# Two transformer blocks on one core: the second buffer of transposed activations at the same offset within 512 bytes as the first

## Chip, core and metric

One core of a Trainium2 chip runs the whole program as one launch. The metric is the device time of that core in microseconds (us). All operands are fp32 in memory. The engines are named as in the profile: PE is TensorE (matmuls), PEld its weight loads, DVE is VectorE, ACT is ScalarE, POOL is GpSimd, SP is SyncE, whose queue issues the DMAs.

## What is computed

256 tokens of width 2048 go through three layers. What matters here are the dense products, since they fill PE:

```python
def _layer(x, ...):                      # first block
    proj = rmsnorm(x) @ w_in             # 2048 -> 2560, then attention and a state space mixer
    x = x + mixed @ w_out                # 2048 -> 2048
    return x + (silu(h2 @ w_ff_gate) * (h2 @ w_ff_up)) @ w_ff_down     # hidden 5632

def second_block(x, ...):                # two more layers
    mix = gmlp_shortconv_mixer(hn, w_in_ab, ..., w_out_ab)             # layer 0: 2048 -> 5120 -> 2048
    mix = dilated_attention_mixer(hn, w_qkv, w_o, positions)           # layer 1
    h = h + rmsnorm(mix, ...)
    f = jnp.square(jax.nn.relu(rmsnorm(h, ...) @ w_up)) @ w_down       # both layers, hidden 8192
    h = h + rmsnorm(f, ...)
```

## The kernel before

**Split products.** Each fp32 product is made of three fp32r matmuls on split operands. A weight tile of 128 rows by 1024 columns is loaded into `RAW` (3 slots of two such tiles, `NRAW`), ACT rounds it into `HI` (L576) and DVE writes the rest into `LO` (L1063), both with 3 slots (`NSPLIT`). The activations are split likewise: they are transposed on PE (L1909, `feed`), ACT writes the rounded part and DVE the rest into a buffer of transposed activations.

**Two such buffers.** `KPA` and `KPB` have the same shape, 128 partitions by 16 chunks by 2 parts (rounded, rest) by 256 tokens, 32768 bytes a partition. `KPA` holds what goes into the products of the normed input (`w_in`, gate and up, `w_in_ab`, `w_qkv`, `w_up`), into `w_glu` and into the state space half of the first `w_out`. `KPB` holds what goes into the products that lead back to the stream: the attention half of the first `w_out`, `w_ff_down`, `w_out_ab`, `w_o` and `w_down`. For the hidden layers `KPB` is used as two halves, chunks 0 to 7 and chunks 8 to 15, in turn (blocks `hid1.b` and `hid2.layer.b`, even and odd b), and the program alternates: one `up` unit from `KPA`, then two `dn` units from `KPB`.

**One step.** `matmuls(u, i)` (L1860 to L1888) does chunk i of unit u: for each of the two tiles t of 128 tokens the three products rounded x HI, rounded x LO, rest x HI, each with 512 columns for the two halves j of the 1024, so 12 matmuls a step (8 read HI, 4 read LO; all are L1884). The 128x128 activations are the stationary operand, one piece of 512 bytes a partition at `buffer + 2048*chunk + 1024*part + 512*t`; the weights `HI`, `LO` are the moving operand, 2048 bytes a partition. A step needs one tile of HI, one of LO and half a DMA of 1 MB.

**Order.** Each engine's instructions are written out in program order by Python generators; semaphores join them. ACT and DVE run ahead of PE by two steps (`LA`) and then wait for a slot of HI or LO. Nothing in the order depends on addresses.

**Layout.** `build` places the SBUF tensors one behind the other from `SBUF_FROM` (16512) up, each rounded up to 64 bytes; the bytes under 16384 are a scratch area that the program builder reserves for descriptors of DMAs generated in software. In bytes of a partition, with the offset within 512 behind: `XR` 16512 (128), `KPA` 32896 (128), `RAW` 65664 (128), `HI` 90240 (128), `LO` 102528 (128), `ACC` 114816 (128), then small ones (`PAR`, `ID`, `ST`, `NEG5`, `LAM`), whose sizes are not multiples of 512, `KPB` 134912 (256), and behind it from `ph_at` 167680 (256) the area that the stages share (`HS`, `JK`, `RL`, `GPF`, `q2T`, `k2T`, `LG`, `PT`, `CL` and others). `BLT` and the bias tables lie inside `KPB`'s bytes while it is not in use.

Of the kernel before, what the change touches and what calls it, by code (L numbers as in the profile page):

```python
# [21 lines left out]
NRAW = 3  # L22
NSPLIT = 3
LA = NSPLIT - 1
SBUF_FROM = 16512
SBUF_TO = 229344


# [268 lines left out]
def program(nc, inp, out, scratch):  # L297
    plan = Plan(inp)
    with ExitStack() as ctx:
        build(nc, ctx, plan, inp, out, scratch)  # L300


def build(nc, ctx, plan, inp, out, scratch):
    S = Semaphores(nc, ctx)
    PS = ctx.enter_context(nc.psum_tensor("PS", [128, 8, 512], F32))
    U, G = plan.by_name, plan.groups
    at = [SBUF_FROM]

    def sb(name, shape, dt=F32, where=None):
        w = where if where is not None else at  # L310
        n = 4
        for d in shape[1:]:
            n *= d
        h = nc.alloc_sbuf_tensor_at(name, list(shape), dt, offset=w[0])
        w[0] += -(-n // 64) * 64
        assert w[0] <= SBUF_TO, (name, w[0])
        return h

    XR = sb("XR", [128, 2, D])
    kpa_at = at[0]  # L320
# [7 lines left out]
    ST = sb("ST", [128, 384])  # L328
    NEG5 = sb("NEG5", [128, 48])
    LAM = sb("LAM", [128, 3, 32])  # L330
    kb = [at[0]]
    ph_at = at[0] + 32768
    BLT = sb("BLT", [128, 4, 2, 8, 128], where=kb)
# [21 lines left out]
    PHI = sb("PHI", [128, 2, 512], where=third)  # L355
    xr_again = [SBUF_FROM]
    LANE = [[sb(f"LANE{p}{i}", [128, 512], where=xr_again) for i in range(2)] for p in range(2)]
# [71 lines left out]
    sp = {n: SPR[:, i, :] for i, n in enumerate("mag qf fre fim dt ang v1 v2 v3 v4 v5 v6 q4".split())}  # L429
    lre, lim, rho = (LAM[:, i, :] for i in range(3))  # L430

# [2023 lines left out]
```

## Time and profile before

| | |
|---|---|
| median of 3 runs | 3388.08 us (3386.37 to 3388.2) |
| the profiled execution, its own time | 3388.41 us |
| its span in the trace | 3386.3 us |
| PE busy | 3273.7 us, 97% |
| DVE, ACT, POOL busy | 1866.3, 1475.8, 119.8 us |
| DMA | 596.28 MB, mean 176 GB/s |

The span is the stretch that the trace covers; the run's time has 2.1 us more around it. Ends of matmuls are modelled in the trace, so a matmul's duration (some 390 ns) is longer than its share of PE: the time that one takes from PE is the distance from its start to the next one's start, which is called pace here.

### The profile page before, as it was taken

To read this page: it belongs to the slowest core of one execution; us is meant where nothing else is said; L and a number is where in the kernel's file an instruction comes from. 1 tells how busy PE (TensorE), PEld (TensorE's weight loads), DVE (VectorE), ACT (ScalarE), POOL (GpSimd) and SP (SyncE) were. 2 spreads that over 40 slices of the span, in tenths; PEclk is the share of its full clock that TensorE was granted. 3 is DMA by queue.
4 is the path that set the end of the run, shared out by engine and by line. 5 is a ranking of instruction groups with operands and counts; after the bars stand their busy time and mean duration, and the time that the engine had idled before them with its cause. 6 is when DMAs were issued, how large, how long until landed. Compare 5 with 4: busy or idle time off the path is not lost. (4 is left out here: it accounts for less than half of the span.)

```text
span 3386.3 us, 38632 instructions
## 1 busy us (share of the span) xinstructions
PE 3273.7 (97%) x15842; PEld 2670.4 (79%) x15842; DVE 1866.3 (55%) x1958; ACT 1475.8 (44%) x1760; POOL 119.8 (4%) x99
## 2 busy tenths in 40 slices
PE   6988999999999999999999999999999999999998
PEld 5776788888888778878888888878787788888886
DVE  6455655555555544665555555565555655555555
ACT  5434444444444444444444444444444544444443
POOL 4230000000000000000000000000000000000000
PEclk9998999999999999999999999999999999999999
DMA  7233455555555555555555555545454555555554
GB/s 200 93 119 121 159 187 186 188 188 193 189 186 187 181 172 188 194 174 180 191 188 190 186 187 186 185 156 186 149 174 154 173 184 186 187 187 187 187 188 146
DMA packets 187548, 596.28 MB, mean 176 GB/s; under 512 B 12491, under 2 KB 19308, under 8 KB 186860
## 3 DMA queue, kind: packets, MB, share of 16 engines
q1 hardware_dynamic: 187372, 593.82, 53.9%
q8 instruction: 125, 2.05, 0.2%
q14 instruction: 51, 0.42, 0.0%
HBM read 588.54 MB, written 5.23 MB: 175 GB/s over the span
## 5 line engine op out<-in xcount | busy, mean ns | idle before, releaser
L1063 DVE TENSOR_TENSOR LO<-RAW,HI 128x1024 fp32r<-128x1024 f32 (+1 forms) x1104 | 1351.6, 1226 | 1183.2 <-ACT HI L576 1181.4
L576 ACT ACTIVATE HI<-RAW 128x1024 fp32r<-128x1024 f32 (+1 forms) x1104 | 1159.2, 1052 | 1396.5 <-PE PS L1884 1392.1
L1884 PE MATMUL PS<-HI,KPA 128*128 128x512 f32 x5376 | 1499.4, 395 | 18.0 <-issue 5.3
L1884 PEld LDWEIGHTS PS<-HI,KPA 128*128 128x128 f32 x5376 | 1008.5, 190 | 233.4 <-issue 15.8
L1884 PE MATMUL PS<-HI,KPB 128*128 128x512 f32 x3392 | 954.9, 397 | 3.9 <-DVE ACC L1559 3.3
L1884 PE MATMUL PS<-LO,KPA 128*128 128x512 f32 x2688 | 841.4, 394 | 9.9 <-DVE LO L1063 9.8
L1884 PEld LDWEIGHTS PS<-HI,KPB 128*128 128x128 f32 x3392 | 631.6, 188 | 150.5 <-issue 5.2
L1884 PEld LDWEIGHTS PS<-LO,KPA 128*128 128x128 f32 x2688 | 509.0, 190 | 122.2 <-DVE LO L1063 11.9
L1884 PE MATMUL PS<-LO,KPB 128*128 128x512 f32 x1696 | 533.9, 395 | 0.8 <-DVE KPB L1099 0.8
L1884 PEld LDWEIGHTS PS<-LO,KPB 128*128 128x128 f32 x1696 | 318.8, 188 | 77.5 <-issue 1.2
L603 ACT ACTIVATE KPB<-PS 128x512 fp32r<-128x512 f32 x98 | 58.6, 599 | 185.0 <-PE PS L1909 185.0
L1094 DVE TENSOR_TENSOR KPB<-PS,KPB 128x512 fp32r<-128x512 f32 x98 | 67.7, 692 | 124.2 <-ACT KPB L603 124.2
L1727 POOL TENSOR_TENSOR ST<-ST,NEG 128x2 f32<-128x2 f32 (+2 forms) x15 | 19.8, 1322 | 2909.7 <-DVE ST L1106 2909.5
L1099 DVE SCALAR_TENSOR_TENSOR KPA<-PS,PAR,KPA 128x256 fp32r<-128x256 f32 x104 | 45.3, 479 | 61.2 <-ACT KPA L608 61.1
L1557 DVE TENSOR_TENSOR ACC<-PS,ACC 128x1024 f32<-128x1024 f32 x60 | 70.7, 1216 | 8.8 <-PE PS L1884 8.8
L608 ACT ACTIVATE KPA<-PS,PAR 128x256 fp32r<-128x256 f32 x104 | 43.3, 470 | 61.2 <-PE PS L1909 60.8
L1909 PE MATMUL PS<-ID,XR 128*128 128x128 f32 x192 | 33.7, 304 | 24.8 <-DVE XR L1591 15.6
L1618 DVE TENSOR_TENSOR HS<-RL 128x1024 f32<-128x1024 f32 x32 | 39.2, 1226 | 25.6 <-ACT RL L979 23.9
L1909 PEld LDWEIGHTS PS<-ID,XR 128*128 128x128 f32 x192 | 26.3, 156 | 33.0 <-DVE XR L1591 19.2
L1909 PEld LDWEIGHTS PS<-ID,HS 128*128 128x128 f32 x344 | 42.8, 140 | 12.0
L1909 PE MATMUL PS<-ID,HS 128*128 128x128 f32 x344 | 51.5, 272 | 0.0
L979 ACT ACTIVATE RL<-PS,ST 128x1024 f32<-128x1024 f32 x32 | 35.8, 1119 | 27.5 <-DVE HS L1618 22.7
(255 smaller groups left out, 988.2 us busy)
## 6 DMA issues: line engine op xcount, KB each, us to landing
RAW<-in_w_up SPq DMA_DIRECT2D x128, 1024.0 KB, 5.1
RAW<-in_w_down SPq DMA_DIRECT2D x128, 1024.0 KB, 5.5
RAW<-in_w_qkv SPq DMA_DIRECT2D x48, 1024.0 KB, 5.1
RAW<-in_w_ff_gate SPq DMA_DIRECT2D x88, 512.0 KB, 3.7
RAW<-in_w_ff_up SPq DMA_DIRECT2D x88, 512.0 KB, 4.6
RAW<-in_w_ff_down SPq DMA_DIRECT2D x44, 1024.0 KB, 5.5
RAW<-in_w_in_ab SPq DMA_DIRECT2D x40, 1024.0 KB, 5.0
RAW<-in_w_in SPq DMA_DIRECT2D x16, 1024.0 KB, 6.2
```

Source lines behind the costliest of these rows:

```text
L576: e.activation(HI[:, s % NSPLIT, 0:w], RAW[:, d % NRAW, j, 0:w], ACT.Copy).then_inc(S("hi_made"), 1)
L603: e.activation(kt[:, ks:ks + 2, 0, :], PS[:, bank, :].rearrange("p (a b) -> p a b", a=2), ACT.Copy).then_inc(S("chunk_hi"), 1)
L608: ins = e.activation(kt[:, ks + c, 0, :], PS[:, bank, c * 256:c * 256 + 256], ACT.Copy, scale=par(g.gain, 2 * j + c, 1))
L979: e.activation(RL[:, :], flat2(b), ACT.Relu, scale=r[:, t:t + 1]).then_inc(S("evac_act"), 1)
L1063: e.tensor_tensor(LO[:, h, 0:w], RAW[:, d % NRAW, j, 0:w], HI[:, h, 0:w].bitcast(F32), ALU.subtract).then_inc(S("lo_made"), 1)
L1094: e.tensor_tensor(kt[:, ks:ks + 2, 1, :], PS[:, bank, :].rearrange("p (a b) -> p a b", a=2), kt[:, ks:ks + 2, 0, :].bitcast(F32), ALU.subt ...
L1099: ins = e.scalar_tensor_tensor(out=kt[:, ks + c, 1, :], in0=PS[:, bank, c * 256:c * 256 + 256], scalar=par(g.gain, 2 * j + c, 1), in1=kt[: ...
L1557: ins = e.tensor_tensor(d, flat2(b), d, ALU.add)
L1618: e.tensor_tensor(HS[b % 2][:, t, :], RL[:, :], RL[:, :], ALU.mult).then_inc(S("squared_relu"), 1)
L1727: e.tensor_tensor(dst, src, NEG5[:, 0:n], ALU.pow).then_inc(S("root_made"), 1)
L1884: ins = e.matmul(PS[:, b + j, 0:cw], l, r[:, h, 512 * j:512 * j + cw], start=(i == 0 and part == 0), stop=(last and part == 2))
L1909: ins = e.transpose(PS[:, bank, c * 256 + t * 128:c * 256 + t * 128 + 128], src(2 * j + c, t), ID[:, :])
```

## The change

It gives the scratch area 4096 bytes in place of 16384, starts the kernel's tensors 12288 bytes lower (from 16512 to 4224), and spends 384 of the bytes that this frees on moving `KPB` up to the same offset within 512 bytes as `KPA`. No instruction, wait or DMA is added, removed or put elsewhere; only addresses differ, and line numbers (L1884 is then L1886).

```diff
-SBUF_FROM = 16512
+SCRATCH = 4096
+SBUF_FROM = SCRATCH + 128
 SBUF_TO = 229344
@@
     NEG5 = sb("NEG5", [128, 48])
     LAM = sb("LAM", [128, 3, 32])
+    at[0] += (kpa_at - at[0]) % 512
     kb = [at[0]]
     ph_at = at[0] + 32768
     BLT = sb("BLT", [128, 4, 2, 8, 128], where=kb)
@@
-    nc = _bacc.Bacc("TRN2", target_bir_lowering=False, num_devices=1)
+    nc = _bacc.Bacc("TRN2", target_bir_lowering=False, num_devices=1, dynamic_dma_scratch_size=SCRATCH)
```

What it makes of the addresses (bytes of a partition, offset within 512 behind):

| tensor | before | after |
|---|---|---|
| XR | 16512 (128) | 4224 (128) |
| KPA | 32896 (128) | 20608 (128) |
| RAW | 65664 (128) | 53376 (128) |
| HI | 90240 (128) | 77952 (128) |
| LO | 102528 (128) | 90240 (128) |
| ACC | 114816 (128) | 102528 (128) |
| ID | 132288 (192) | 120000 (192) |
| KPB | 134912 (256) | 123008 (128) |
| shared area, from ph_at | 167680 (256) | 155776 (128) |

After it `KPA`, `HI`, `LO` and `KPB` also have the same offset within 4096 bytes (128); before, `KPB` had 3840 there and the others 128.

## Rows read from the trace of the kernel before

**Rows 1.** The page: span, busy time by engine, granted clock in 40 slices.
```profile
span 3386.3 us, 38632 instructions
...
PE 3273.7 (97%) x15842; PEld 2670.4 (79%) x15842; DVE 1866.3 (55%) x1958; ACT 1475.8 (44%) x1760; POOL 119.8 (4%) x99
...
PEclk9998999999999999999999999999999999999999
```
**Rows 2.** Groups by line and shape: count, busy us, mean ns, idle before and releaser.
```profile
L1063 DVE TENSOR_TENSOR LO<-RAW,HI 128x1024 fp32r<-128x1024 f32 x1088 | 1337.9, 1232 | 1163.8 <-ACT HI L576 1162.0
L576 ACT ACTIVATE HI<-RAW 128x1024 fp32r<-128x1024 f32 x1088 | 1149.2, 1059 | 1367.9 <-PE PS L1884 1363.5 <-DMA RAW<-in_w_in 4.5
...
L1618 DVE TENSOR_TENSOR HS<-RL 128x1024 f32<-128x1024 f32 x32 | 39.2, 1226 | 25.6 <-ACT RL L979 23.9 <-PE PS L1884 1.7
```
**Rows 3.** The view of line L1884: count, shortest/median/longest duration in ns.
```profile
L1884 PE MATMUL PS<-HI,KPA x5376: 387/389/797, 10.3 to 3280.6; 128*128 128x512 f32 x200
...
L1884 PE MATMUL PS<-HI,KPB x3392: 387/395/763, 369.8 to 3371.9; 128*128 128x512 f32 x200
...
L1884 PE MATMUL PS<-LO,KPA x2688: 387/389/796, 11.5 to 3280.2; 128*128 128x512 f32 x192
...
L1884 PE MATMUL PS<-LO,KPB x1696: 390/393/628, 371.3 to 3371.5; 128*128 128x512 f32 x189
```
**Rows 4.** Timeline of PE in an up unit: start us, length us, what.
```profile
1060.12 1.07 PE L1884 MATMUL PS<-HI,KPA 128*128 128x512 f32 x4
...
1068.28 1.07 PE L1884 MATMUL PS<-HI,KPA 128*128 128x512 f32 x4
```
**Rows 5.** The same in a dn unit on chunks 8 to 15 of KPB.
```profile
1881.98 1.10 PE L1884 MATMUL PS<-HI,KPB 128*128 128x512 f32 x4
...
1894.58 1.10 PE L1884 MATMUL PS<-HI,KPB 128*128 128x512 f32 x4
```
**Rows 6.** The same in a dn unit on chunks 0 to 7 of KPB.
```profile
1790.52 1.10 PE L1884 MATMUL PS<-HI,KPB 128*128 128x512 f32 x4
...
1804.52 1.10 PE L1884 MATMUL PS<-HI,KPB 128*128 128x512 f32 x4
```
**Rows 7.** The same in the unit wa1, chunks 0 to 7 of KPB.
```profile
385.31 1.09 PE L1884 MATMUL PS<-HI,KPB 128*128 128x512 f32 x4
...
395.06 1.09 PE L1884 MATMUL PS<-HI,KPB 128*128 128x512 f32 x4
```
**Rows 8.** The same where an up unit ends and a dn unit begins.
```profile
1085.96 1.07 PE L1884 MATMUL PS<-HI,KPA 128*128 128x512 f32 x4
...
1087.32 0.62 PE L1884 MATMUL PS<-HI,KPA 128*128 128x512 f32 x2
1087.78 0.64 PE L1884 MATMUL PS<-HI,KPB 128*128 128x512 f32 x2
1088.25 0.62 PE L1884 MATMUL PS<-LO,KPB 128*128 128x512 f32 x2
```
**Rows 9.** Chain that ended last, one piece: the two units of w_o without transposes.
```profile
2593.90 44.89 PE PS L1884 x192
```
**Rows 10.** Stretches of an up unit and a dn unit: busy, PEclk, DMA share, GB/s.
```profile
1750.00:1760.00 10.00, 10.00 (x46) 8.29 (x45) 4.90 (x4) 3.67 (x4) 0.00 (x0) 1.00 0.56 175
...
1885.00:1895.00 10.00, 10.00 (x44) 8.06 (x43) 4.24 (x4) 4.24 (x4) 0.00 (x0) 1.00 0.56 175
```
**Rows 11.** The view of line L1909, transposes from the shared area and from XR.
```profile
L1909 PE MATMUL PS<-ID,HS x344: 270/272/273, 472.1 to 3299.3; 128*128 128x128 f32 x172
...
L1909 PE MATMUL PS<-ID,XR x192: 270/273/474, 6.5 to 2678.5; 128*128 128x128 f32 x192
```
**Rows 12.** The page, DMA queues: packets, MB, share of 16 engines.
```profile
q1 hardware_dynamic: 187372, 593.82, 53.9%
q8 instruction: 125, 2.05, 0.2%
q14 instruction: 51, 0.42, 0.0%
```

## The prediction

> **What bounds the kernel now.** I read the page first. PE is busy for 3273.7 of the 3386.3 us of the span, DVE and ACT for about half, and the granted clock is at its upper level (2.4 GHz) in nearly every slice [rows 1]. The groups say the same from the other side: DVE's LO instructions stood idle for 1163.8 us until ACT's HI was there, and ACT's HI for 1363.5 us until a matmul of L1884 had freed a slot [rows 2]. So the stream of dense matmuls sets the time, and ACT, DVE and the weight DMAs follow it. A saving on a dense matmul is then a saving on the run, as long as those three keep up.
>
> A change that only moves addresses can act there only by the time that one matmul takes. The view of the line shows a first trace of that: the median duration is 389 ns with KPA as the stationary operand and 395 (HI) or 393 (LO) with KPB, though all four groups do the same work [rows 3]. Durations have modelled ends, so I go on to the timeline and take the distance between starts. One half of a step is 6 matmuls, from one "HI x4" row to the next.
> - up unit on KPA, no other PE work between: (1068.28 - 1060.12) / 36 = 226.7 ns [rows 4].
> - dn unit on chunks 8 to 15 of KPB: (1894.58 - 1881.98) / 54 = 233.3 ns [rows 5]; on chunks 0 to 7: (1804.52 - 1790.52) / 60 = 233.3 ns [rows 6].
> - unit wa1 on KPB: (395.06 - 385.31) / 42 = 232.1 ns [rows 7].
> - the two w_o units without transposes, as a whole: (44.89 - 0.39) / 191 = 233.0 ns; 0.39 is the length of the last matmul [rows 3, 9].
>
> So each matmul whose stationary operand lies in KPB costs some 6 ns more. The clock is no part of it: it is 1.00 in both kinds of stretch, and DMA share (0.56) and GB/s (175) are alike [rows 10]. Nor is a late input: no row of these stretches has an idle time before it. At a border the pace goes over with the operand itself: up to 1087.32 the last 6 matmuls on KPA take 1.36 us, and the first 2 on KPB, with HI and LO made in the same way and the same work on ACT and DVE, take 0.47 us, 235 ns each [rows 8].
>
> **The change part by part.**
>
> *KPB from offset 256 to offset 128 within 512.* KPB is the stationary operand of 3392 + 1696 = 5088 dense matmuls [rows 3]. What tells KPB from KPA in the program is its address alone: shape, steps between pieces and type are the same, and HI and LO are read in the same way. In address, two things differ: the offset within 512 (256 against 128, with all of HI, LO, RAW at 128), and where in the partition it lies. The change takes the first difference away, and not the second. If the pace follows the offset, all 5088 go from 233.0 to 226.7 ns: 5088 x 6.3 ns = 32.1 us, all of it on PE, which sets the end. The bounds are 5.4 ns (232.1 - 226.7, rows 7), 27.5 us, and 6.6 ns (233.3 - 226.7, rows 5 and 6), 33.6 us. I take the value of rows 9 since it is that of whole units, not of a picked stretch.
>
> That piece of reasoning rests on rows alone, and a rule speaks against it. The Trainium skill says that TensorE has two independent read ports in SBUF, so that loading the next weights takes nothing from the running matmul (TensorE: Matmul & The Clock Gate, Step-by-step), that "PE and ACT never wait on anyone" (SBUF — State Buffer, Who interferes with whom), and that what counts for an access is its 16-byte line (the same page, the box on cachelines of Door 1); 128 and 256 are both multiples of 16. By these the offset could cost nothing and the sum would be 0 in place of -32.1. Against the trace that holds only half: the rule has no place for 233 beside 227, which the rows show, so something in the address does cost. It is kept as a rival below.
>
> *Will the others keep up?* At 226.7 ns a step of 12 matmuls lasts 2.72 us in place of 2.80. ACT needs 1.06 us a step and DVE 1.23 [rows 2] beside their other work: 4.24 us of 10 each in the dn stretch [rows 10]. The up units run at that pace already, on the same weight bytes a step, with the same slots. So HI and LO don't come late, and nothing else is next: the 32 us are not handed on. What would be lost were the cover gone: 0.08 us a step, which is the gain itself.
>
> *Everything else down by 12288 bytes.* XR, KPA, RAW, HI, LO, ACC keep their offset within 4096, and so their offsets to each other: no cost. KPA's 8064 matmuls [rows 3] keep 226.7 ns unless the place in the partition counts.
>
> *The shared area from 256 to 128.* PE reads it for the transposes of HS and others, and the nearest rows with an operand at 128 are those of XR: 272 against 273 ns, for 344 and 192 instructions [rows 11]. Bound: within 1 ns either way, 0.3 us for HS, under 1 us with the other transposes and attention products. DVE takes 1226 ns on HS and RL, both at 256, and 1232 ns on tensors that are all at 128 [rows 2]; both are off the path. I count 0, with 1 us either way.
>
> *The scratch area from 16384 to 4096 bytes.* All weight and activation traffic is on the hardware queue q1; beside it there are only instruction fetches [rows 12]. No queue uses the scratch. 0 us.
>
> Sum: the profiled execution took 3388.4 us by its own time, span 3386.3 and 2.1 around it, which is 0.3 over the median of the runs shown, 3388.1. From the two, 3388.4 - 32.1 = 3356.3 and 3388.1 - 32.1 = 3356.0; I write 3356.5, leaning a little to the smaller saving of rows 7. Own range of this case: 3388.1 - 33.6 - 2 = 3352.5 to 3388.1 - 27.5 + 1 = 3361.6.
>
> **The rivals.**
> - *Nothing changes.* The slow pace comes from where KPB lies (far up, behind HI and LO) or from the kind of stage, not from the offset; by the skill's rules cited above it would be this case too. For it: KPB stays above ACC, and rows 5 to 9 can't part offset from place. Against it: KPB covers 32 KB from 134912 on, and its lower and its upper half have the same pace to 0.1 ns [rows 5, 6], so a dependence on place would have to be one that is flat over all of it; and the border in rows 8 rules out the stage. Time: 3388.1. That is also the time if the changed placement doesn't do what it says.
> - *A part of the gain.* Place counts in large blocks and the slow block begins at 131072, a round address just under the old KPB. Then of the new KPB, from 123008 on, the first (131072 - 123008) / 2048 = 3.9 of 16 chunks become fast: 32.1 x 3.9 / 16 = 8 us, 3380. For it only that the old KPB lies wholly above that line; against it, that nothing in the trace shows a line at all.
> - *Slower.* The same kind of block, but at 32768: KPA now lies wholly above it (32896) and after the change begins at 20608, so that (32768 - 20608) / 2048 = 5.9 of its 16 chunks come under it. If pieces there have KPB's pace, 8064 x 5.9 / 16 x 6.3 ns = 19 us more, and KPB gains nothing since the offset is not the cause: 3407. It decides from the point where the lost time on KPA is over the gain on KPB; if offsets count after all, the sum is still -13. Against it: again no line in the trace, and KPB crosses 163840, a multiple of 32768, in the trace without a step in pace [rows 5, 6].
>
> **How the numbers follow.** Forecast 0.77, a part of the gain 0.05, nothing 0.12, slower 0.06. The forecast gets that much because the loss is visible, is tied to the operand by rows 8, and the change makes KPB equal to KPA in the only respect that varies finely; what remains is that two buffers can't part offset from place. The range takes in the forecast's own range and the partial case, 0.82 together: 3351 to 3381. A measurement of this kernel can tell about 0.2% from no change, 6.8 us. Faster by more than that is under 3381.3: 0.82. Within it 0.12, slower 0.06.
>
> **What would show it.** Right: in the view of the dense line, KPB's median duration falls from 395 and 393 ns to 389, that of KPA stays 389; the distance of "HI x4" rows in dn units falls from 1.40 to 1.36 us; the w_o piece of 192 from 44.89 to about 43.7 us; the span by about 32 us, spread over all dn, oab, wa and wo units and none of it in up units; ACT's and DVE's busy times stay, their idle times shrink. Wrong: dn units still at 1.40 us (place or stage); some chunks fast and others not (blocks); up units over 1.36 us (KPA hurt); dn units at 1.36 us but gaps before PE rows that wait for HI, LO or the DMAs (the cover fails).

## The result

The changed kernel takes 3356.3 us (median of 4 runs, 3355.07 to 3357.21), the kernel before 3388.14 us beside it (median of 4, 3386.37 to 3389.04): a ratio of 0.9906, 95% interval 0.9889 to 0.9924, 31.8 us less. Its profiled execution has a span of 3353.9 us, 32.4 less than before.

The page of after, the lines that answer to [rows 1]:

```profile
span 3353.9 us, 38632 instructions
...
PE 3243.4 (97%) x15842; PEld 2668.1 (80%) x15842; DVE 1866.0 (56%) x1958; ACT 1475.7 (44%) x1760; POOL 119.7 (4%) x99
...
PEclk9998999999999999999999999999999999999999
```

PE's busy time went from 3273.7 to 3243.4, and the instruction counts, DVE's, ACT's and POOL's busy time and the granted clock are as they were. The view of the dense line (now L1886) answers to [rows 3]:

```profile
L1886 PE MATMUL PS<-HI,KPA x5376: 387/389/797, 10.3 to 3250.6; 128*128 128x512 f32 x200
...
L1886 PE MATMUL PS<-HI,KPB x3392: 387/389/628, 366.1 to 3339.6; 128*128 128x512 f32 x200
...
L1886 PE MATMUL PS<-LO,KPB x1696: 387/389/628, 367.7 to 3339.1; 128*128 128x512 f32 x189
```

KPB's median durations, 395 and 393 ns, are 389 ns now, KPA's. The timeline of PE in the dn unit on chunks 8 to 15 (start us, length us, what), which answers to [rows 5], and under it a stretch of an up unit, as [rows 4]:

```profile
1864.03 1.07 PE L1886 MATMUL PS<-HI,KPB 128*128 128x512 f32 x4
...
1878.99 1.07 PE L1886 MATMUL PS<-HI,KPB 128*128 128x512 f32 x4
```
```profile
1047.95 1.07 PE L1886 MATMUL PS<-HI,KPA 128*128 128x512 f32 x4
...
1058.83 1.07 PE L1886 MATMUL PS<-HI,KPA 128*128 128x512 f32 x4
```

From one such row to the next are 6 matmuls: (1878.99 - 1864.03) / 66 = 226.7 ns on KPB, (1058.83 - 1047.95) / 48 = 226.7 ns on KPA. The two w_o units without transposes, as [rows 9], in the chain that ended last:

```profile
2571.70 43.82 PE PS L1886 x192
```

44.89 us before, 43.7 forecast. What ACT and DVE make for the next step still waits for PE and not the other way round: DVE's LO stood idle 1134.8 us for ACT's HI, ACT's HI 1337.8 us for PE (1162.0 and 1363.5 in [rows 2]); each lost 26 to 27 us of idle time, which is where the shorter steps show up on them:

```profile
L1065 DVE TENSOR_TENSOR LO<-RAW,HI 128x1024 fp32r<-128x1024 f32 x1088 | 1337.8, 1232 | 1136.6 <-ACT HI L578 1134.8
L578 ACT ACTIVATE HI<-RAW 128x1024 fp32r<-128x1024 f32 x1088 | 1149.5, 1059 | 1342.4 <-PE PS L1886 1337.8 <-DMA RAW<-in_w_in 4.4
```

### The profile page after: what moved, and what is told of

It is laid out like the page before. It is cut to its first block and busy times, and to the rows that moved or that the text cites. A ratio compares the mean times of both kernels' runs of the same rounds, so it can differ in the third digit from the quotient of the medians.

```text
span 3353.9 us, 38632 instructions
## 1 busy us (share of the span) xinstructions
PE 3243.4 (97%) x15842; PEld 2668.1 (80%) x15842; DVE 1866.0 (56%) x1958; ACT 1475.7 (44%) x1760; POOL 119.7 (4%) x99
## 5 line engine op out<-in xcount | busy, mean ns | idle before, releaser
L1886 PE MATMUL PS<-HI,KPA 128*128 128x512 f32 x5376 | 1499.3, 395 | 18.4 <-issue 5.3
L1886 PEld LDWEIGHTS PS<-HI,KPA 128*128 128x128 f32 x5376 | 1008.8, 190 | 233.5 <-issue 16.6
L1886 PE MATMUL PS<-HI,KPB 128*128 128x512 f32 x3392 | 935.4, 392 | 4.0 <-DVE ACC L1561 3.4
L1886 PE MATMUL PS<-LO,KPA 128*128 128x512 f32 x2688 | 841.6, 394 | 9.8 <-DVE LO L1065 9.7
L1886 PEld LDWEIGHTS PS<-HI,KPB 128*128 128x128 f32 x3392 | 631.1, 188 | 133.0 <-issue 5.3
L1886 PEld LDWEIGHTS PS<-LO,KPA 128*128 128x128 f32 x2688 | 509.3, 190 | 121.8 <-DVE LO L1065 12.0
L1886 PE MATMUL PS<-LO,KPB 128*128 128x512 f32 x1696 | 524.3, 390 | 0.8 <-DVE KPB L1101 0.8
L1886 PEld LDWEIGHTS PS<-LO,KPB 128*128 128x128 f32 x1696 | 318.5, 188 | 68.8 <-issue 1.2
```

What stands on the lines that cost most here:

```text
L1886: ins = e.matmul(PS[:, b + j, 0:cw], l, r[:, h, 512 * j:512 * j + cw], start=(i == 0 and part == 0), stop=(last and part == 2))
```

## The experiments

All are edits of the changed kernel. Where tensors are pushed apart, `acc_at`, a base that is worked out from `kpa_at`, moves by the bytes put in; that line, and the ones that pick a piece of a cut buffer or put what lies behind back, are left out of the cuts where they aren't shown. A pace is the distance from one matmul's start to the next one's, in stretches of one unit without other work of PE.

### Offset or place

The prediction had left open whether KPB's offset or its place in the partition made it slow. The first kernel keeps the new place (to 384 bytes) and takes the alignment out; the second keeps the alignment and nearly the old place (KPB at 134784, before 134912).

```diff
-    at[0] += (kpa_at - at[0]) % 512
```

> The changed kernel without its alignment line: all tensors lie 12288 bytes lower, KPB at 122624, offset 256 within 512. Theory (the offset between stationary and moving operand within 512, or the offset as such): KPB matmuls keep the slow pace of 233.3 ns, the run takes 3388 us. Rival (the place in the partition): KPB at 226.7 ns and 3356 us, or something between.

Measured: 3386.7 us (median of 10 runs, 3382.6 to 3390.8), ratio to before 0.9998 (0.9989 to 1.0008). Timeline of PE in a dn unit: (1894.23 - 1883.03) / 48 = 233.3 ns.

```profile
1883.03 1.10 PE L1885 MATMUL PS<-HI,KPB 128*128 128x512 f32 x4
...
1894.23 1.10 PE L1885 MATMUL PS<-HI,KPB 128*128 128x512 f32 x4
```

```diff
-SBUF_FROM = SCRATCH + 128
+SBUF_FROM = 16000
```

> The alignment with nearly the old places: tensors start at 16000 (512 lower than before), KPB at 134784 (128 lower than before), offset 128. Theory (offset): KPB at 226.7 ns, 3356 us. Rival (place): KPB at 233.3 ns, 3388 us.

Measured: 3356.5 us (median of 4), ratio 0.9908 (0.9891 to 0.9924), pace (1878.87 - 1867.99) / 48 = 226.7 ns.

```profile
1867.99 1.07 PE L1886 MATMUL PS<-HI,KPB 128*128 128x512 f32 x4
...
1878.87 1.07 PE L1886 MATMUL PS<-HI,KPB 128*128 128x512 f32 x4
```

So the whole gain comes from the one line that aligns, and the 12288 bytes of shift only make room for it; 512 of them are enough, as the second kernel shows. The rivals of place (nothing, a part, slower) fall.

### The offset as such, or the distance to the other operand

```diff
-SBUF_FROM = SCRATCH + 128
+SBUF_FROM = SCRATCH + 256
```

> The changed kernel moved up by 128 bytes as a whole: XR, KPA, RAW, HI, LO, ACC, KPB and the shared area all at offset 256 within 512. If the offset between stationary and moving operand counts, all dense matmuls stay at 226.7 ns and the run takes 3356 us. If the offset of the stationary operand as such counts, all 13152 go to 233.3 ns: KPA's 8064 add 8064 x 6.6 ns = 53 us and KPB's 5088 add 34 us, 3443 us.

Measured: 3356.8 us (median of 4), ratio 0.9911 (0.9896 to 0.9926); pace on KPB, now at 256 as in the kernel before, (1878.81 - 1866.57) / 54 = 226.7 ns.

```profile
1866.57 1.07 PE L1886 MATMUL PS<-HI,KPB 128*128 128x512 f32 x4
...
1878.81 1.07 PE L1886 MATMUL PS<-HI,KPB 128*128 128x512 f32 x4
```

```diff
-SBUF_FROM = SCRATCH + 128
+SBUF_FROM = SCRATCH + 64
```

> The changed kernel 64 bytes lower as a whole: all large tensors at offset 64 within 512. Theory (only the distance between the operands within 256 counts): 226.7 ns and 3356 us. Rival (128 and 256 are both good places as such, 64 is not): up to 233 ns, 3440 us.

Measured: 3355.2 us (one run), pace (1877.65 - 1866.77) / 48 = 226.7 ns.

```profile
1866.77 1.07 PE L1886 MATMUL PS<-HI,KPB 128*128 128x512 f32 x4
...
1877.65 1.07 PE L1886 MATMUL PS<-HI,KPB 128*128 128x512 f32 x4
```

The offset as such doesn't matter; three common offsets (64, 128, 256) give one pace. Then it must be the distance between the stationary operand (KPA, KPB) and the moving one (HI, LO), or between KPA and KPB. The next kernel moves HI and LO alone and puts what is behind them back:

```diff
+    at[0] += 128
     HI = sb("HI", [128, NSPLIT, 1024], F32R)
     LO = sb("LO", [128, NSPLIT, 1024], F32R)
+    at[0] += 384
```

> The changed kernel with HI and LO both moved up by 128 bytes, KPA and KPB at 128 as in it. Theory (the offset between the operands counts): all 13152 dense matmuls go to 232.5 to 233.3 ns, 13152 x 5.8 to 6.6 ns = 76 to 87 us more, 3432 to 3443 us. Rival (KPA and KPB must match each other, not HI and LO): 3356 us.

Measured: 3419.0 us (one run, 3386.8 before beside it), 62.7 us over the changed kernel. KPA and KPB still match each other, and both are slow: in an up unit (1088.01 - 1062.92) / 108 = 232.3 ns.

```profile
1062.92 1.09 PE L1888 MATMUL PS<-HI,KPA 128*128 128x512 f32 x4
...
1088.01 1.10 PE L1888 MATMUL PS<-HI,KPA 128*128 128x512 f32 x4
```

The pair that counts is stationary and moving. ACT and DVE use HI and LO at the same addresses, so a clash of PE with one of them was a rival. The trace of the kernel before speaks against it: in its units between 1740 and 2120 us, a matmul on KPB takes 233.3 ns while ACT alone works beside PE and 233.1 while DVE alone does, one on KPA 226.7 and 226.8 (means of single starts). No stretch is without both, so it isn't shut out altogether. The time is under the 3432 to 3443 expected: the pace is a little better than the 232.5 to 233.3 that I had put in, and not every matmul pays in full (below).

### How the pace depends on the distance

KPB is cut into eight tensors of two chunks, each at another offset (the shared area behind them moved up to make room). HI and LO are at 128, so the distances, stationary less moving, are -128, -64, 0, 64 and so on up to 320 bytes:

```diff
-    KPB = nc.alloc_sbuf_tensor_at("KPB", [128, 16, 2, 256], F32R, offset=at[0])
+    KPB = [nc.alloc_sbuf_tensor_at(f"KB{'ABCDEFGH'[i]}", [128, 2, 2, 256], F32R, offset=at[0] - 128 + i * 4096 + 64 * i)
+           for i in range(8)]
```

> The changed kernel with KPB cut in eight tensors of two chunks each, KBA to KBH, at the offsets 0, 64, 128, ... 448 within 512; HI, LO, KPA stay at 128. So each product from KPB goes over four offsets (even hidden blocks over 0 to 192, odd ones over 256 to 448). Theory (the offset sets the pace, finer than as a yes or no): KBC (128) at 226.7 ns, KBE (256) at 233.3 ns, the others somewhere between 220 and 245 ns, each steady; the run between 3330 and 3420 us. Rival (only exact equality helps): KBC alone at 226.7, the other seven at 233.3 ns. Rival (only a large block of addresses counts): a single step of pace somewhere along KBA to KBH.

Measured: 3373.0 us (one run). Timeline of PE, second unit of an even and of an odd block; only the rows in which the operand changes are left. Each piece has two steps, 24 matmuls.

```profile
1783.36 0.62 PE L1890 MATMUL PS<-HI,KBA 128*128 128x512 f32 x2
...
1788.93 0.63 PE L1890 MATMUL PS<-HI,KBB 128*128 128x512 f32 x2
...
1794.43 0.62 PE L1890 MATMUL PS<-HI,KBC 128*128 128x512 f32 x2
...
1799.89 0.63 PE L1890 MATMUL PS<-HI,KBD 128*128 128x512 f32 x2
...
1805.49 0.62 PE L1890 MATMUL PS<-HI,KPA 128*128 128x512 f32 x2
```
```profile
1873.02 0.62 PE L1890 MATMUL PS<-HI,KBE 128*128 128x512 f32 x2
...
1878.60 0.63 PE L1890 MATMUL PS<-HI,KBF 128*128 128x512 f32 x2
...
1884.10 0.62 PE L1890 MATMUL PS<-HI,KBG 128*128 128x512 f32 x2
...
1889.56 0.63 PE L1890 MATMUL PS<-HI,KBH 128*128 128x512 f32 x2
...
1895.16 0.62 PE L1890 MATMUL PS<-HI,KPA 128*128 128x512 f32 x2
```

The differences, over 24: KBA (offset 0) 232.1 ns, KBB (64) 229.2, KBC (128) 227.5, KBD (192) 233.3; KBE (256) 232.5, KBF (320) 229.2, KBG (384) 227.5, KBH (448) 233.3. The second four repeat the first four to 0.4 ns. The pattern has a period of 256 bytes, not 512, and each offset has its own pace. (KBC and KBG have 226.7 ns inside and lose 0.8 on average at the border from a slower piece.) The rival of exact equality within 512 falls with KBG, that of a large block with the order of the pieces. A whole kernel at that distance:

```diff
-    at[0] += (kpa_at - at[0]) % 512
+    at[0] += (kpa_at + 256 - at[0]) % 512
```

> The changed kernel with KPB at offset 384 within 512, KPA, HI and LO at 128: unequal within 512, equal within 256. In the run with eight offsets the piece at 384 had 226.7 ns for two steps at a time. Theory (the period is 256 bytes): all of KPB at 226.7 ns, 3356 us. Rival (512, as the change has it, and the piece at 384 only profited from its neighbours): slow pace, 3380 to 3388 us.

Measured: 3356.0 us (median of 4), ratio 0.9909 (0.9892 to 0.9925), pace on KPB (1878.63 - 1867.75) / 48 = 226.7 ns. The kernel before was 128 bytes from the fast place.

```profile
1867.75 1.07 PE L1886 MATMUL PS<-HI,KPB 128*128 128x512 f32 x4
...
1878.63 1.07 PE L1886 MATMUL PS<-HI,KPB 128*128 128x512 f32 x4
```

Then the same cut with small distances, to see whether a better one than 0 exists; each piece is a view at an inner offset of a wider tensor (their allocation is left out):

```diff
+    KPB = [b[:, 16 + d // 4:16 + d // 4 + 1024].rearrange("p (a b c) -> p a b c", a=2, b=2)
+           for b, d in zip(KPB, (-48, -32, -16, 16, 32, 48, 0, 8))]
```

> As the run with eight offsets, but with KBA to KBH at -48, -32, -16, +16, +32, +48, 0 and +8 bytes against HI and LO within 256. In that run equal offsets gave 226.7 ns, +64 gave 233.3, +128 gave 232.5, +192 (-64) gave 228.8. Theory (equal is the best there is): KBG 226.7 ns, all others above it, rising with the distance, quicker on the positive side. Rival (the best lies beside equal, since it is a matter of phase): one of the others is under 226.7 ns, say 222. Either way the run is within 3350 to 3385 us.

Measured: 3380.0 us (one run). The timeline, read as above:

```profile
1789.32 0.62 PE L1892 MATMUL PS<-HI,KBA 128*128 128x512 f32 x2
...
1794.89 0.62 PE L1892 MATMUL PS<-HI,KBB 128*128 128x512 f32 x2
...
1800.48 0.64 PE L1892 MATMUL PS<-HI,KBC 128*128 128x512 f32 x2
...
1805.98 0.63 PE L1892 MATMUL PS<-HI,KBD 128*128 128x512 f32 x2
...
1811.58 0.62 PE L1892 MATMUL PS<-HI,KPA 128*128 128x512 f32 x2
```
```profile
1890.31 0.62 PE L1892 MATMUL PS<-HI,KBG 128*128 128x512 f32 x2
...
1895.77 0.62 PE L1892 MATMUL PS<-HI,KBH 128*128 128x512 f32 x2
...
1901.31 0.62 PE L1892 MATMUL PS<-HI,KPA 128*128 128x512 f32 x2
```

-48 bytes 232.1 ns, -32 232.9, -16 229.2, +16 233.3, 0 227.5 with its border, +8 230.8; +32 and +48 have 233.3 each. None is under distance 0. Eight bytes up are enough to lose 3 to 4 ns, 16 bytes up to be at the worst pace; 16 bytes down lose only 2.5. It doesn't rise steadily with the distance, as was expected: -64 (229.2) is better than -32, and -48 (232.1) too.

### Which matmuls pay

```diff
     HI = sb("HI", [128, NSPLIT, 1024], F32R)
+    at[0] += 128
     LO = sb("LO", [128, NSPLIT, 1024], F32R)
+    at[0] += 384
```

> The changed kernel with LO alone moved up by 128 bytes (offset 256 within 512, ACC and all behind it back at their offsets). Theory (what counts is the offset between the stationary piece that is being loaded and the moving operand that is streamed meanwhile): only the matmuls around those that stream LO become slow, 4 of 12, so some 4384 x 6.6 ns = 29 us, 3385 us; and the two intervals that begin with a LO matmul grow (load of the next piece under a stream of LO), not those that end with one. Rival (a matmul pays for its own pair of operands before it starts): the intervals that end at a LO matmul grow instead. Rival (only the pair KPA or KPB with HI counts): 3356 us.

Measured: 3403.5 us (one run), more than the 3385 expected. Timeline of PE in a dn unit:

```profile
1886.84 0.62 PE L1888 MATMUL PS<-LO,KPB 128*128 128x512 f32 x2
1887.30 1.08 PE L1888 MATMUL PS<-HI,KPB 128*128 128x512 f32 x4
1888.22 0.62 PE L1888 MATMUL PS<-LO,KPB 128*128 128x512 f32 x2
...
1894.23 1.08 PE L1888 MATMUL PS<-HI,KPB 128*128 128x512 f32 x4
```

The pace is (1894.23 - 1887.30) / 30 = 231.0 ns over all matmuls, and the four that stream HI, whose distance is still 0, take 1888.22 - 1887.30 = 0.92 us, 230 ns each, with 226.7 in the changed kernel. One of these four intervals ends at a LO matmul, and the rows are rounded, but the single starts in the trace say the same (means of 76 half steps of dn units between 1740 and 2120 us): the interval from the second to the third HI matmul, which touches no LO matmul, is the longest, 235.9 ns against 226.3 in the changed kernel, while the three that begin or end at one have 231.6 to 232.6. So the cost does not stay with the matmuls that stream the displaced operand, and both pictures that I had of when it is paid (while the next stationary piece is loaded, or before a matmul's own start) were too simple. Which of the two reads waits for which, and why, stays open.

```diff
     XR = sb("XR", [128, 2, D])
+    at[0] += 64
     kpa_at = at[0]
     KPA = sb("KPA", [128, 16, 2, 256], F32R)
+    at[0] += 448
```

> The changed kernel with KPA alone moved up by 64 bytes (offset 192; HI, LO, KPB and the rest at 128). Theory: KPA's 8064 matmuls go to 233.3 ns, KPB stays at 226.7: 8064 x 6.6 ns = 53 us if every one of them counts, 3409 us. The run with HI and LO moved gave +62.9 us of span for 13152 matmuls at about 232.8 ns, 4.8 ns each and not 5.5 to 6, so I expect less than the full product here too: 45 to 53 us, 3401 to 3409 us. Rival (a loss on KPA is hidden, since up units have other waits): under 30 us.

Measured: 3400.8 us (one run), 44.5 us over the changed kernel, just under the 3401 to 3409 expected. KPA has 8064 matmuls, so this is 5.5 ns each, though the stretches show the full (1070.64 - 1062.24) / 36 = 233.3 ns:

```profile
1062.24 1.10 PE L1888 MATMUL PS<-HI,KPA 128*128 128x512 f32 x4
...
1070.64 1.10 PE L1888 MATMUL PS<-HI,KPA 128*128 128x512 f32 x4
```

I took the time of each stage from the first dense matmul on one buffer to the first on the other. A dense up stage of 192 matmuls grows from 43.5 to 44.8 us (6.6 ns each), the stage of w_qkv and the second attention with its waits (1152 matmuls) from 299.3 to 304.7 us, 4.7 ns each. Of the 2.2 us that are missing there, a wait takes up only 0.6 (PE's idle time falls from 8.2 to 7.6 us). About 1.1 us more is at the transposes: a matmul in the 11 places behind a group of them takes 230.1 ns in the changed kernel and 233.5 here, the others 228.0 and 234.6 (means of single starts). So next to transposes the distance costs about half.

### The transposes

```diff
-    PAR = sb("PAR", [128, NPAR])
     ID = sb("ID", [128, 128])
+    PAR = sb("PAR", [128, NPAR])
```

> The changed kernel with the identity ID (the other operand of the transposes) at offset 128 within 512, where XR and the shared area are, in place of 192. If the rule for the dense matmuls holds for the 128-column transposes too, their distance of 108.6 ns falls by a few ns, 800 x 3 ns = 2.4 us, 3354 us. Rival (a transpose is set by the load of 128 columns, not by the stream, so nothing is there to gain): 3356 us, distance still 108.6 ns.

Measured: 3356.1 us (median of 4), ratio 0.9905 (0.9888 to 0.9921): the changed kernel's time. Four transposes of HS still take 0.35 to 0.36 us to the next dense row, as before, and from one transpose to the next are 108.3 ns (108.8 in the changed kernel, 108.5 before):

```profile
1001.89 0.60 PE L1911 MATMUL PS<-ID,HS 128*128 128x128 f32 x4
1002.25 0.71 PE L1886 MATMUL PS<-HI,KPB 128*128 128x512 f32 x2
```

The 2.4 us hoped for would hardly show in times that scatter by 7 us; the distance says that nothing is to be had there. No kernel of this study beats the changed one beyond the scatter: 3356.0 to 3356.8 for all that have distance 0 within 256 and several runs.

## Why the prediction was right, and which term was off

**The bound, right.** PE's dense stream sets the time; a few ns on each of 5088 matmuls came out at the end, since the stages that use KPB are 28.3 us shorter in sum and the run is 31.8 us shorter; ACT and DVE only lost idle time.

**The reading of the pace, right.** KPB's pace went to exactly KPA's. That two buffers alone can't part offset from place was the gap in the argument; the pair of runs on place and alignment closes it. The reason that the prediction gave was too narrow in one point and too wide in another: it spoke of an offset of KPB within 512, and the runs show a distance to HI and LO, within 256.

**The rule that spoke against it.** The Trainium skill's independent read ports and "PE and ACT never wait on anyone" (SBUF — State Buffer, Who interferes with whom) would have given no change. The runs with HI and LO moved, with KPA moved and with eight offsets all show PE's pace following the addresses of its own two operands, 226.7 to 233.3 ns. Nor does the 16-byte line, which the prediction took from that page, explain it: distances of 16, 32 and 48 bytes are whole lines and cost up to 6.6 ns, and -64 costs less than -32.

**The saving, right to 0.3 us in sum, but by two terms that were each off, which is luck.** The stages on KPB together took 1269.3 us before and 1241.0 after (by the same starts as above, the last stage up to its last matmul on KPB): 28.3 us, 5.6 ns a matmul, where the prediction had 6.3 and 32.1. The step that failed is the price. It set 233.0 ns, a whole unit with the start after a wait, against 226.7 ns, a picked clean stretch. Like against like, [rows 9] give 44.89 - 43.82 = 1.07 us for 192, 5.6 ns. And a dn stage with transposes, from its first matmul on KPB to the next on KPA, begins before at 1768.28 and ends at 1814.78, after:

```profile
1753.20 0.61 PE L1886 MATMUL PS<-HI,KPB 128*128 128x512 f32 x2
...
1798.66 0.62 PE L1886 MATMUL PS<-HI,KPA 128*128 128x512 f32 x2
```

46.50 against 45.46 us, 5.4 ns each, though the clean stretches of the same stage differ by the full 233.3 - 226.7 = 6.6. The rest is lost behind the transposes, where the changed kernel doesn't reach 226.7. From the first dense matmul behind a group of transposes to the next group are 12:

```profile
1777.00 0.71 PE L1884 MATMUL PS<-HI,KPB 128*128 128x512 f32 x2
...
1779.89 0.60 PE L1909 MATMUL PS<-ID,HS 128*128 128x128 f32 x4
```
```profile
1761.72 0.71 PE L1886 MATMUL PS<-HI,KPB 128*128 128x512 f32 x2
...
1764.58 0.60 PE L1911 MATMUL PS<-ID,HS 128*128 128x128 f32 x4
```

2.89 us before and 2.86 after, 2.5 ns each. The lower bound, from wa1 [rows 7], 27.5 us, was the nearest to the 28.3 us of the stages.

The other 4.1 us of the span's 32.4 is almost all in the first stage, where nothing was forecast (the later stages on KPA give 0.3 us): the first matmul on KPB starts at 369.8 us before [rows 3] and at 366.1 after. The runs do not tie that to the addresses. The same start is at 373.9 us without the alignment, and with it at 373.6 (old place), 372.1 (all at 256), 365.1 (256 apart):

```profile
L1885 PE MATMUL PS<-HI,KPB x3392: 387/393/767, 373.9 to 3374.4; 128*128 128x512 f32 x200
```
```profile
L1886 PE MATMUL PS<-HI,KPB x3392: 387/389/632, 373.6 to 3344.6; 128*128 128x512 f32 x200
```

The granted clock explains a part: over the first 366 us it is 0.90 to 0.91 in the three that start latest (372.1 to 373.9 us), 0.93 before and with KPB 256 apart, 0.94 after. Of the 3.7 us between before and after, 1.5 are a single group of 128 matmuls (L1956, after it L1958): it lasts 5.2 us before, where the clock from 105 to 120 us is 0.89, and 3.7 us after, where it is 1.00. Most of the rest is PE's wait for ACT's `BLT`: 16.2 us before, 13.6 after, and between 12.1 and 15.2 in the other kernels at distance 0. What makes that wait differ is open.

So one profiled execution says 32.4 where the stages that changed say 28.3. The medians of repeated runs of the five kernels at distance 0 lie 30.4 to 31.8 us under before's beside them, while the runs of one kernel scatter by 2 to 8 us. So 28.3 us are placed, and the last 2 to 3.5 us of the medians are not: they may be scatter, or a small gain in the first stage that the starts can't show. The forecast of 3356.5 against 3356.3 was helped by that: the stages alone would have made it about 3360, still within the range.

**The rest, right.** Nothing else was late at 2.72 us a step, the transposes from the shared area stayed at 272 ns, and the scratch area has no user here.

## What to carry to other kernels

Where PE is full, compare the pace of the same matmul with different operands, from start to start in the timeline: medians of duration 389 against 395 ns were the first sign here, and 0.9% of the kernel. If they differ, compare addresses before anything else, stationary against moving operand, and try the same offset within 256 bytes for both. The runs show this for fp32r matmuls of 128x512 with a weight load ahead of each; 128-column transposes gained nothing, and other shapes and types were not tried. When you price such a difference, take both paces from the same kind of stretch, and check a result by the stages that changed rather than by the span, with the granted clock beside it.

## What the runs showed of the hardware

- The pace of a 128x512 fp32r matmul, with a load of 128x128 ahead of each, depends on the distance between its stationary and moving operands in the partition: 226.7 ns at 0, 232.1 to 233.3 ns at most others, 230.8 ns at 8, 229.2 ns at -16 and -64, with a period of 256 bytes. The common offset has no influence (64, 128, 256).
- The loss isn't even. In the dn units of the kernel before, the two matmuls of a pair on one stationary piece start 237 ns apart, and the next pair 229 ns after that (means of 76 half steps); on KPA all are within 1 ns of 226.7.
- If only a third of the matmuls stream an operand at another distance, all of them get slower: 231.0 ns.
- Behind a group of transposes the price is smaller: a dense step there takes 2.89 us at 128 bytes and 2.86 at 0, where a clean one takes 2.80 and 2.72.
- The same 128 bytes gave 233.3 ns in the dn units of the kernel before, 232.1 in its wa1 unit [rows 7], and 232.1 to 232.5 ns in pieces of two steps and with HI and LO moved. What makes that difference is open.
